# A rotary turn made of ScalarE block copies in place of a TensorE product

## What is computed

```python
def apply_rope(x, cos, sin):
    xr = x.reshape(b, s, h, 2, 2, d // 4)
    x1, x2 = xr[..., 0, :], xr[..., 1, :]
    out = stack([x1 * cs - x2 * sn, x1 * sn + x2 * cs], axis=-2)
# per layer (the rest of the block: mLSTM, short convolution, gates, merge, squared-relu MLP)
aq = apply_rope(rms_norm(heads(p[5], 8), q_norm), cos, sin)      # latent tokens only
ak = apply_rope(rms_norm(heads(p[6], 2), k_norm), cos, sin)
softmax(aq @ [ak_ctx, ak].T * 128 ** -0.5) @ [av_ctx, av]
```

## Time and profile before

| | |
|---|---|
| time, median of 3 runs | 1839.8 us (1839.62 to 1840.02) |
| the profiled execution: time / span | 1842.64 us / 1840.9 us |
| mean granted TensorE clock | 0.994 of full speed |
| busy share PE / DVE / ACT / POOL | 98% / 57% / 39% / 10% |

### The profile page before, as it was taken

The page is one execution under the profiler, slowest core; times in us unless marked ns, Lnnn a source line. Parts: engine busy times, 40 slices in busy tenths (PEclk is TensorE's granted clock), DMA queues, the critical chain, the costliest instruction groups (busy, mean ns, idle before and its releaser), DMA issues.

```text
span 1840.9 us, 24988 instructions
## 1 busy us (share of the span) xinstructions
PE 1809.6 (98%) x10187; PEld 1552.5 (84%) x10187; DVE 1052.0 (57%) x1538; ACT 724.9 (39%) x1011; POOL 177.7 (10%) x178
## 2 busy tenths in 40 slices
PE   7999998999999999999999999999999999999998
PEld 4887787888888888878888888788999999999997
DVE  5435635555556665466675655645657556566555
ACT  3425434444222322343232323344546544445444
POOL 2100101011110101320000000200110110020000
PEclk9999999999999999999999999999999999999999
DMA  9221121112444453536444536233243375575553
GB/s 310 92 92 46 41 84 59 57 58 69 142 151 142 137 166 109 166 132 205 138 138 137 174 101 189 64 115 93 68 126 104 115 252 184 184 229 170 194 186 115
DMA packets 214290, 245.55 MB, mean 133 GB/s; under 512 B 5836, under 2 KB 186400, under 8 KB 214176
## 3 DMA queue, kind: packets, MB, share of 16 engines
q1 hardware_dynamic: 213872, 243.85, 41.0%
q10 hardware_dynamic: 304, 0.10, 0.0%
HBM read 242.89 MB, written 1.05 MB: 133 GB/s over the span
## 4 chain that ended last, share of the span: by engine, by line
PE 78%; DVE 2%; ACT 1%; issue 1%; DMA 0%; POOL 0%; DVEq 0%; ACTq 0%
PE pp L1214 17%; PE pp L1218 16%; PE pp L1215 16%; PE pp L1222 4%; PE pp L1221 4%; PE pp L1223 4%; PE pc L1105 2%; PE pc L1104 2%; PE pc L1106 2%; PE pc L1411 1%; PE pp L1146 1%; PE pp L1147 1%; PE pp L1145 1%; PE pc L1483 1%; PE pc L1318 1%
## 5 line engine op out<-in xcount | busy, mean ns | idle before, releaser
L1990 DVE TENSOR_TENSOR wL<-raw,wH 128x1024 fp32r<-128x1024 f32 (+1 forms) x360 | 441.6, 1268 | 356.8 <-ACT wH L1527 354.8
L1214 PE MATMUL pp<-hH,wH 128*128 128x512 f32 (+1 forms) x1708 | 570.3, 344 | 0.4 <-ACT hH L1748 0.3
L1215 PE MATMUL pp<-hH,wL 128*128 128x512 f32 (+1 forms) x1708 | 561.2, 339 | 0.0
L1527 ACT ACTIVATE wH<-raw 128x1024 fp32r<-128x1024 f32 x360 | 361.0, 1051 | 454.4 <-DMA raw<-in_w_in 201.3
L1218 PE MATMUL pp<-hL,wH 128*128 128x512 f32 (+1 forms) x1708 | 439.9, 339 | 2.1 <-POOL hL L1921 1.5
L1214 PEld LDWEIGHTS pp<-hH,wH 128*128 128x128 f32 x1708 | 324.1, 190 | 42.8 <-issue 8.3
L1215 PEld LDWEIGHTS pp<-hH,wL 128*128 128x128 f32 x1708 | 324.3, 190 | 35.2 <-issue 1.0
L1218 PEld LDWEIGHTS pp<-hL,wH 128*128 128x128 f32 x1708 | 294.5, 190 | 38.9 <-POOL hL L1921 2.8
L1222 PE MATMUL pp<-yL,wH 128*128 128x512 f32 (+1 forms) x320 | 114.3, 357 | 0.0
L1221 PE MATMUL pp<-yH,wH 128*128 128x512 f32 (+1 forms) x320 | 114.3, 357 | 0.0
L1223 PE MATMUL pp<-yH,wL 128*128 128x512 f32 (+1 forms) x320 | 114.2, 357 | 0.0
(11 more groups left out here) (286 smaller groups left out, 2346.5 us busy)
## 6 DMA issues: line engine op xcount, KB each, us to landing
raw<-in_w_in SPq DMA_DIRECT2D x83, 1024.0 KB, 5.2
raw<-in_w_up SPq DMA_DIRECT2D x32, 1024.0 KB, 5.4
raw<-in_w_down SPq DMA_DIRECT2D x32, 1024.0 KB, 5.1
pair_W<-in_w_ada SPq DMA_DIRECT2D x10, 2048.0 KB, 8.0
ada_Y<-in_w_ada SPq DMA_DIRECT2D x10, 1024.0 KB, 11.1
ada_H<-in_w_ada SPq DMA_DIRECT2D x8, 1024.0 KB, 12.2
raw<-in_w_proj_m SPq DMA_DIRECT2D x8, 1024.0 KB, 5.1
raw<-in_w_proj_a SPq DMA_DIRECT2D x8, 1024.0 KB, 5.1
```

The costliest lines, as they stand in the source:

```text
L1214: pe.matmul(dsts[b], wh[b], hi[:, kt, ts_], start=first, stop=False)
L1215: pe.matmul(dsts[b], wl[b], hi[:, kt, ts_], start=False, stop=False)
L1527: act.activation(wH[:, p % HIGH, a:a + KH, :], raw[place_of[p]][:, a:a + KH, :], ACT.Copy).then_inc(wH_ready, 1)
L1990: dve.tensor_tensor(wL[place_of[p]][:, ks, :], raw[place_of[p]][:, ks, :], wH[:, p % HIGH, ks, :].bitcast(F32), ALU.subtract).then_inc(wL_ ...
```

## The change

The rotary turn has no TensorE product any more. ScalarE copies the latent tokens of the two heads in four blocks of 32 partitions to the swapped places of `q_turned`, and the sign of the turn goes into the sine table. `BACK = [1, 0, 3, 2]` is the order of the blocks. VectorE multiplies `q_turned` by the signed sines in place. Since ScalarE's copies stand in its own queue at each `qrot` step, before the key rounding at `qrot` 2, they wait for the turn before them (`qk_ready`). In `gate` 0, `qss` 4 now stands behind six k-tiles (layer 1: four); before it stood behind two. In layer 1 it uses bank 0.

```diff
-    rot = np.zeros((P, P), np.float32)
...
-    return np.concatenate([ident, row_sum, rot, np.cos(ang), np.sin(ang), sel, one_row, pair_row],
+    return np.concatenate([ident, row_sum, np.cos(ang), np.where(d[:, None] % 64 < 32, -1, 1) * np.sin(ang), sel, one_row, pair_row],
...
-                part(kind, l, c, b, 0, 2, split=True)
+                part(kind, l, c, b, 0, 6 if more else 4, split=True)
                 step("qss", l, j=4)
-                part(kind, l, c, b, 2, 4)
                 if more:
                     step("qrot", l, j=4)
-                part(kind, l, c, b, 4, 6)
+                part(kind, l, c, b, 6 if more else 4, 7 if more else 6)
...
         elif k == "qss":
-            use(st, 0, 3)
+            use(st, 0, 0 if st["j"] == 4 and st["l"] else 3)
...
-        elif k == "qrot":
-            use(st, 0, 2 if st["j"] < 3 or st["j"] == 3 and st["l"] else 3)
...   (TensorE)
-                elif k == "qrot":
-                    j = st["j"]
-                    if j:
-                        pe.wait_ge(aqk_in, l * 5 + j + 1)
-                    else:
-                        pe.wait_ge(kn_ready, l + 1)
-                    b = claim(u[0])
-                    for b_ in range(NB):
-                        src = k_a[:, b_, CTX:TOK] if j == 0 else q_a[:, 2 * (j - 1) + b_, CTX:TOK]
-                        last = pe.matmul(b[:, b_ * LAT:(b_ + 1) * LAT], rot, src, start=True, stop=True)
-                    filled(last, u[0])
...   (ScalarE)
-                elif k == "qrot" and st["j"] == 2:
-                    act.wait_ge(qk_ready, l * 5 + 2)
-                    act.activation(kH[:, :, :], k_a[:, :, :], ACT.Copy).then_inc(kH_ready, 1)
-                    round_query(l, 0)
+                elif k == "qrot":
+                    j = st["j"]
+                    if j:
+                        act.wait_ge(aqk_in, l * 5 + j + 1)
+                    else:
+                        act.wait_ge(kn_ready, l + 1)
+                    n = l * 5 + qk_order.index(j)
+                    if qk_order.index(j) == 0:
+                        act.wait_ge(y_ready, y_no[l, "m", MH - 1] + 1)
+                    if n:
+                        act.wait_ge(qk_ready, n)
+                    src = k_a if j == 0 else q_a[:, 2 * j - 2:2 * j, :]
+                    for blk in range(4):
+                        to, of = 32 * blk, 32 * BACK[blk]
+                        act.activation(q_turned[l][to:to + 32, :, :], src[of:of + 32, :, CTX:TOK], ACT.Copy
+                                       ).then_inc(turned_ready, 1)
+                    if j == 2:
+                        act.wait_ge(qk_ready, l * 5 + 2)
+                        act.activation(kH[:, :, :], k_a[:, :, :], ACT.Copy).then_inc(kH_ready, 1)
+                        round_query(l, 0)
...   (VectorE)
-                    b, q_t = bank(dve, u[0]), q_turned[l]
+                    q_t = q_turned[l]
+                    dve.wait_ge(turned_ready, 4 * (l * 5 + qk_order.index(j) + 1))
...
-                        i = dve.tensor_tensor(q_t[:, b_, :], b[:, b_ * LAT:(b_ + 1) * LAT], ropeS, ALU.mult)
-                        if b_ < NB - 1:
-                            start_link(i)
-                        else:
-                            freed(i, u[0])
+                        start_link(dve.tensor_tensor(q_t[:, b_, :], q_t[:, b_, :], ropeS, ALU.mult))
```

More of the change, by code:

```diff
@@ L67, in make_constants @@
     ident = np.eye(P, dtype=np.float32)
-    rot = np.zeros((P, P), np.float32)
-    for m in range(P):
-        if m % 64 < 32:
-            rot[m + 32, m] = -1.0
-        else:
-            rot[m - 32, m] = 1.0
     nf = AHD // 4
@@ L104 @@
 C_WIDE = C_AT + 32
-CONST_COLS = FIRST_COLS + P + LAT + LAT + 40 + 8 + 8
+CONST_COLS = FIRST_COLS + LAT + LAT + 40 + 8 + 8
 def spans(l, d, s):
@@ L703, in trunk @@
         ars = at("ars", [P, 4], F32, o); o += 32
-        ident, row_sum, rot = con[:, 0:P], con[:, P:FIRST_COLS], con[:, FIRST_COLS:FIRST_COLS + P]
+        ident, row_sum = con[:, 0:P], con[:, P:FIRST_COLS]
         pair_row = con[:, CONST_COLS - 8:CONST_COLS]
-        ropeC, ropeS = (con[:, FIRST_COLS + P + i * LAT:FIRST_COLS + P + (i + 1) * LAT] for i in range(2))
-        sel = con[:, FIRST_COLS + P + 2 * LAT:CONST_COLS - 16]
+        ropeC, ropeS = (con[:, FIRST_COLS + i * LAT:FIRST_COLS + (i + 1) * LAT] for i in range(2))
+        sel = con[:, FIRST_COLS + 2 * LAT:CONST_COLS - 16]
         pp = ctx.enter_context(nc.psum_tensor("pp", [P, 2, NB, TOK], F32))
@@ L803, in trunk @@
         vH_ready = sem("vH_ready")
+        turned_ready = sem("turned_blocks_ready")
         kH_ready = sem("kH_ready")
@@ L2423, in _ @@
                     dve.wait_ge(dchain, count[0])
-                    dve.wait_ge(free[u[0][0]], u[0][1] + 1)
                     start_link(dve.tensor_tensor(dst[0], dst[0], q_t[:, 0, :], ALU.add))
```

## The result

The changed kernel takes 1844.4 us (median of 13 runs, 1842.75 to 1846.58), the one before 1839.8 (13 runs, 1838.42 to 1842.54). The ratio is 1.0022, with a 95% interval of 1.0014 to 1.0031: slower, by about the least that a measurement tells from no change. 1837.0 was forecast, with a range to 1841.5. The profiled execution of after took 1846.25 us, 3.6 more than that of before (1842.64).

What follows compares the result with a forecast made beforehand. TensorE, busy 98% of the span, was taken as the bound. Layer 0 at -8.7 and layer 1 at +5.9 us gave -2.8 on the profiled 1842.64; the median, 2.8 lower, was forecast at 1837.0, range 1832.5 to 1841.5.

Steps and rivals of the forecast that it cites:

- The places of the waits: TensorE would wait about 1.6 and 6 us before scores 0, about 4 and 2 before scores 1; qss 4 without wait.
- The split by layer: Layer 0 would end 8.7 us ahead of the kernel before, layer 1 5.9 us behind it.
- The removed product's 0.86 us: Each rotary product taken off TensorE saves 0.86 us; ten of them 8.6 us, 4.3 us a layer.
- spacing of the copies: ScalarE's block copies follow each other every 0.55 us, so four end after 2.27 us and hold the queue for 2.2.
- My upper end, 0.62: Largest copy spacing on ScalarE, if copies starting at different partitions can't overlap: about -7.9 + 6.7 = -1.2 us (1838.6).
- my sum for the spacing of 0.52: With ScalarE copies at the lower-end spacing: -9.1 + 5.4 = -3.7 us, 1836.1 us.
- rival 3: ScalarE's block copies are dearer because they move data across partitions: 2.5 us per 0.1 us each, mostly slower; chance 0.10.
- none or a short one: In layer 0 the granted clock at half would be absent or brief at 323 us.
- costs little: Layer 1: TensorE idles 6 us at scores 0 and the clock falls, cheaply, since the next bound is elsewhere.
- the 313.9 of the prediction: In layer 0, the time in us at which TensorE asks for qss 4, its squares being ready at 303.
- Rival 1: The clock falls in layer 0 too, behind the new 3.8 us wait; price 2.3 us, total 1839.3; chance 0.22.

Runs made afterwards that it cites:

- e10: Against the kernel before: layer 0 with copies, two turn buffers, keys' turn ahead of panel aq 2, last two turns behind scores 1 and 3; layer 1 unchanged: 1826.2 us.
- e12: Kernel before, products kept; in layer 0 qss 4 behind six k-tiles, last two turns behind scores 1 and 3, q_turned in its own memory: 1830.6 us.
- e11: Changed kernel with four whole 128-partition copies a turn in place, three to memory nothing reads, block swap left out: 1838.4 us.
- e3_forms: Changed kernel with groups of ScalarE copies of different forms appended, run once for spacing only: 0.52 us apart at the same partitions, 0.65 where the start changes.
- e1: Kernel before with all products kept; only qss 4 moved behind six k-tiles (layer 1: four, bank 0) and layer 0's fourth product behind the seventh: 1832.4 us.
- e7: Changed kernel with two q_turned buffers used in turn, in memory free at that time: 1839.8 us.
- e6: Changed kernel with idle matmuls in layer 1, 50 ahead of scores 0 and 18 ahead of the second half of probs 1: 1841.7 us.
- e5: Changed kernel's layer 0 with layer 1 left as in the kernel before: 1834.7 us.
- e9: Changed kernel with two turn buffers, keys' turn ahead of panel aq 2, kH first, last two turns behind scores 1 and 3, qss 4 in bank 3: 1832.0 us.

## Why the prediction was wrong

**What held.** The places of the waits: `qss` 4 waits no more; `kH` stands behind two groups of copies; `scores` 0 waits 2.5 and 7.0 us in layers 0 and 1 (1.6 and 6 forecast), `scores` 1 2.7 and 1.7 (about 4 and 2), and in layer 1 the second half of `probs` 1 2.8 (1.9). The split by layer was right in sign (-8.7 and +5.9 forecast, -5.5 and +9.2 measured). The removed product's 0.86 us: five of them were worth 4.4 us (e10 against e12), 4.3 by the prediction.

**The first term that failed: spacing of the copies, 0.55 us taken, 0.65 measured.** Four copies last 2.59 us and hold ScalarE for 2.62, not 2.27 and 2.2. I had the right pair of rows, VectorE's step at a change of partitions and ScalarE's copies at one place, and took the one nearer in engine, not the one nearer in what differs. My upper end, 0.62, was the duration without the 0.02 to 0.03 between two instructions that do not overlap. Two groups ahead of `kH` put `scores` 0 of layer 0 at 304.37 in place of 303.5, `scores` 1 at 325.0 in place of 323.5. With copies that overlap the kernel takes 1838.4 (e11); my sum for the spacing of 0.52 said 1836.1. So this term alone does not make the miss. That rival 3 (dearer copies, slower) gave the right direction was luck: its reason, data that move to other partitions, is refuted by e3_forms.

**The second: the clock, "none or a short one" in layer 0, and in layer 1 "costs little".** It fell four times: 17.0 us at the lower level in the two stretches, 10.2 before. Two of the falls cost time.
- In layer 0 the matmuls of `scores` 1 run at half speed and eat 1.5 us (7.2 us ahead at the start of `scores` 1, 5.7 ahead at the exponentials behind it). The stretch between these two takes 4.75 us here, and 3.22, 3.42 and 3.41 in before, e1 and e7, where the clock was full. The fall at 305.0 costs nothing at the exponentials of head 0 (4.61 us from the start of `scores` 0, 5.05 before), but slows the k-tiles: `qss` 4 starts at 316.28 and not at the 313.9 of the prediction, which left no slack behind it (e11).
- In layer 1 "costs little, because the next bound is elsewhere" was right for the fall that it was said of, at `scores` 0 (e6). The prediction had no second fall. The one at 1400.6, in a stage where TensorE is the bound, makes head 3 1.0 us later. Head 2 is 7.4 us late and head 3 8.1, where I had 6.3 and 5.9; what the clock doesn't explain of this lies at head 1 (6.1 late, 5.7 forecast) and in the wait of 2.76 us (1.9 forecast).

The idle matmuls gave back 2.2 to 2.7 us (e6). Rival 1 had this mechanism for layer 0 at 2.3 us, and I gave it 0.22, since I took the stall's length (3.8 against 5.06 us) for the measure. It isn't: waits of 2.49 and 2.69 us stood ahead of the two falls of layer 0.

**What stood in no term.** In layer 1 ScalarE's split for head 7 waits 1.91 us for a load of the weights (0.69 before), another 1.1 us. From head 6 to head 7 the eight kernels with copies in layer 1 and no idle matmuls took 10.6 to 11.0 us; before, e1, e5, e10 and e12 took 9.3 to 9.5, but so did e6, which has the copies. The load is not issued late: it goes out 2.5 us ahead of the exponentials of head 6 before, and 2.7 ahead both in the changed kernel and in e6. It takes longer: 6.5 us from issue to landing in the changed kernel, 5.1 in e6, for the same 1024 KB. Why is open.

**The sum**, by the exponentials: layer 0 3.2 us worse than forecast, about half by the start of `scores` 1 (copies, for the most part) and half by the clock behind it; layer 1 3.3 us worse, 0.4 by head 1, about 1.8 at heads 2 and 3 (1.0 clock, the rest the wait), 1.1 at head 7. The price in rival 3, 2.5 us for each 0.1 us, was too low as well (4.8 to 5.9 for 0.13): it left out the clock, which stood at the lower level for 3.2 us less in e11.

**Layer 1 stays a loss with better places too.** e9 and e10 differ in layer 1 alone, 5.8 us. The exponentials of e9 lose some 1.4 us between head 1 and 2, where the copies of j = 3 stand, and 2.6 between 3 and 4, where those of j = 4 do (12.95 against 11.57 us before, 12.96 against 10.40). Against e10 it is 1.4 and 3.0 there, another 1.2 between heads 0 and 1 and 1.5 at the load for head 7, and 1.2 come back in between. Behind the first group TensorE's timeline has a wait of 1.71 us for the attend copy, and its chain of waits three such, 4.9 us in all. A head of layer 1 takes 9 to 12 us, one of layer 0 16 to 17. That ScalarE has no 2.6 us to spare in front of that copy in the shorter one is my reading of these waits; no run moves these two groups alone.

## What to carry to other kernels

When work goes from a busy engine to an idle one, price it by what stands behind it in that engine's queue, stage by stage: here the same copies were worth +4.4 us in layer 0 once nothing waited behind them, and cost 6 us in layer 1. Before the work is moved at all, try to remove the stall by order alone: two steps of the list moved gave 7 us of the 13.3 that were to be had, with no operation changed. Look at the granted clock behind each new wait, the short ones too, and then ask whether TensorE is the bound in that stage: of the change's four falls two cost 1.5 and 1.0 us, and the other two nothing at the softmax behind them. Before two profiled executions are compared, take out what they differ by in a stage that the change doesn't touch.

## What the runs showed of the hardware

- ScalarE's copies of 512 elements overlap (0.52 us apart, 0.61 long) only when source and target start at the same partitions as those of the one before; otherwise they are 0.65 apart, whether or not the data change partitions, also where only the target's start differs (e3_forms).
- The length of a wait did not tell whether the clock falls. At `scores` 0 of layer 0 it fell with waits of 2.49 us (the change) and 0.33 us (e7_two_buffers, windows over 302 to 308 us: 0.82, 0.50 and 0.82), each behind 16 one-column matmuls. At `scores` 1 of layer 0 it fell with 2.69 us (the change) and stayed at full level with 2.13 (e11_same_place), 1.89 (e7_two_buffers) and 1.24 (e1_move_only).
- Between the layers, where nothing differs between these kernels, the profiled executions spent from 0 to 10.2 us at the lower level (before 6.8, after 6.8, e1_move_only 0, e9_turns_later 10.2), with TensorE busy all through the windows of before over 804 to 812 us, one of which has 0.60. By an estimate that is up to 5 us, half of 10.2, between two traces of kernels that do the same there. The Trainium skill (TensorE: Matmul & The Clock Gate, What's actually happening) says that one and the same kernel has a different number of slow matmuls at its start from run to run. The traces here agree that it varies, in the middle of a kernel.
- VectorE's addition of 0.42 us took 2.46 while GpSimd's `kL` ran beside it (L2418, from 300.68 in the changed kernel), as in the prediction.
